# A token-mixing and expert layer pair in fp32: no receptance for the context, two-bank evictions and a 64x64 transposition in the recurrence

## What is computed

```
pc = modulate(rmsnorm(ctx, norm1_g[l]), csh1, csc1) @ w_in[l]
px = modulate(rmsnorm(x, norm1_g[l]), sh1, sc1) @ w_in[l]
cr, ck, cv, cw, ca, cgl = split_rwkv(pc_rw, shift_mu[l], seq_shift(pc_rw))
xr, xk, xv, xw, xa, xgl = split_rwkv(px_rw, shift_mu[l], grid_shift(px_rw, rows))
yc, sf, sb, rc, kc, vc = rwkv_bidir(cr, ck, cv, cw, ca, ..., s_zero, s_zero)
yx, _, _, rx, kx, vx = rwkv_bidir(xr, xk, xv, xw, xa, ..., sf, sb)
def step(s, inp):                     # 8 heads of 64, forwards and backwards
    r_t, w_t, k_t, v_t, a_t, b_t = inp
    sa = einsum('bhvk,bhk->bhv', s, a_t)
    s = s * w_t[:, :, None, :] + sa[..., :, None] * b_t[:, :, None, :] + v_t[..., :, None] * k_t[:, :, None, :]
    return s, einsum('bhvk,bhk->bhv', s, r_t)
```

## Time and profile before

| | us |
|---|---|
| median of the 3 runs shown | 2326.87 |
| lowest, highest | 2322.07, 2332.89 |
| span of the profiled execution | 2324.3 |
| PE busy in it | 2102.2 (90%) |
| VectorE busy | 1575.8 (68%) |
| ScalarE busy | 1245.2 (54%) |
| projection's products, first to last | 60 to 406 |
| recurrence, first logits to last output | 410 to 853 |

### The profile page before, as it was taken

One profiled execution on the slowest core, in us unless ns is written; L12 is line 12 of the kernel. 1 busy time (PEld: TensorE's weight loads), 2 busy tenths in 40 slices (PEclk: granted clock), 3 DMA queues, 4 the chain that ended last, 5 costly groups with the idle time before them and its releaser, 6 DMA issues. The chain is left out here.

```text
span 2324.3 us, 51473 instructions
## 1 busy us (share of the span) xinstructions
PE 2102.2 (90%) x21654; PEld 1675.4 (72%) x21654; DVE 1575.8 (68%) x2324; ACT 1245.2 (54%) x2324; POOL 659.5 (28%) x465
## 2 busy tenths in 40 slices
PE   5999999599999988891799999999958999999989
PEld 3788888477888853681688888888747778866667
DVE  3666654788889746427599999999766846556531
ACT  4422221476677654433688888888645434357530
POOL 0000020566666610114013323323034455400011
PEclk8999999799999999996899999999979999999999
DMA  8222252333222239426599999999845364230032
GB/s 287 59 68 61 71 130 47 74 72 72 64 64 65 58 110 354 146 100 235 208 354 384 389 397 388 387 395 392 280 132 179 105 221 115 88 131 2 2 110 81
DMA packets 164658, 399.63 MB, mean 172 GB/s; under 512 B 13630, under 2 KB 58060, under 8 KB 164428
## 3 DMA queue, kind: packets, MB, share of 16 engines
q1 hardware_dynamic: 149804, 347.56, 43.0%
q0 software_dynamic: 12224, 44.57, 7.0%
q10 hardware_dynamic: 2400, 4.21, 0.5%
HBM read 348.06 MB, written 46.66 MB: 170 GB/s over the span
## 5 line engine op out<-in xcount | busy, mean ns | idle before, releaser
L1940 DVE TENSOR_TENSOR exp_w_lo<-mixT,exp_w_hi 128x2048 fp32r<-128x2048 f32 x124 | 278.7, 2283 | 23.4 <-ACT exp_w_hi L1897 23.4
L1897 ACT ACTIVATE exp_w_hi<-mixT 128x1024 fp32r<-128x1024 f32 x256 | 255.0, 1053 | 55.8 <-PE banks L1859 38.6
L2153 POOL TENSOR_TENSOR w_lo<-mixT,w_hi 128x512 fp32r<-128x512 f32 (+1 forms) x108 | 145.7, 1370 | 166.6 <-ACT w_hi L2229 163.9
L1859 PE MATMUL banks<-exp_w_hi,xsT_lo 128*128 128x512 f32 x512 | 161.0, 396 | 6.3 <-DVE xsT_lo L1944 6.3
L1859 PE MATMUL banks<-exp_w_lo,xsT_hi 128*128 128x512 f32 x512 | 159.4, 393 | 0.0
L1859 PE MATMUL banks<-exp_w_hi,xsT_hi 128*128 128x512 f32 x512 | 159.3, 393 | 0.0
L1827 POOL DMA_INDIRECT moe_rows<-exp_out,idxT x16 | 25.2, 1573 | 435.7 <-DVE exp_out L1999 435.7
L2211 PE MATMUL banks<-w_hi,h_lo 128*128 128x512 f32 (+1 forms) x320 | 123.5, 386 | 7.8 <-POOL w_lo L2153 5.3
L2211 PE MATMUL banks<-w_lo,h_hi 128*128 128x512 f32 (+1 forms) x320 | 120.3, 376 | 0.0
L2211 PE MATMUL banks<-w_hi,h_hi 128*128 128x512 f32 (+1 forms) x320 | 120.2, 376 | 0.0
L1812 POOL DMA_INDIRECT xs<-xn_rows,idxT x16 | 116.0, 7248 | 14.2 <-DVE idxT L1971 5.6
(11 more groups left out here) (395 smaller groups left out, 5857.7 us busy)
## 6 DMA issues: line engine op xcount, KB each, us to landing
mixT<-in_exp_w_up_dram SPq DMA_DIRECT2D x62, 1024.0 KB, 10.2
mixT<-in_exp_w_gate_dram SPq DMA_DIRECT2D x34, 1024.0 KB, 9.3
mixT<-in_exp_w_down_dram SPq DMA_DIRECT2D x32, 1024.0 KB, 9.2
mixT<-in_w_in_dram SPq DMA_DIRECT2D x96, 256.0 KB, 2.9
ada_w_second<-in_ada_w_dram SPq DMA_DIRECT2D x16, 1024.0 KB, 9.6
kaT<-in_exp_w_down_dram SPq DMA_DIRECT2D x16, 1024.0 KB, 7.1
exp_w<-in_exp_w_down_dram SPq DMA_DIRECT2D x16, 1024.0 KB, 7.4
chunk<-rkv_scratch SPq DMA_DIRECT2D x80, 192.0 KB, 4.0
```

The costliest lines, as they stand in the source:

```text
L1859: mm = pe.matmul(g.ps[bank + q][:, :], lhs[:, kk, :], wide[:, k, q * 512:(q + 1) * 512], start=(kk == 0 and p == 0), stop=(kk == KT - 1 an ...
L1897: last = act.activation(wh[:, n % RH, k, :], w[n % RING][:, k, :], ACT.Copy)
L1940: dve.tensor_tensor(wl[:, n % RH, :, :], w[n % RING], wh[:, n % RH, :, :], ALU.subtract).then_inc(lo_ok, 1)
L2153: pool.tensor_tensor(wl[:, q % SR, 0:width(q)], w[:, q % WR, 0:width(q)], wh[:, q % SR, 0:width(q)], ALU.subtract).then_inc(w_lo, 1)
```

## The change

Five edits, of which the first has two halves:

- r (tiles 0 to 3) and the gate's tile 13 are projected, mixed and stored for the image alone; in the recurrence, chunks of the context load, multiply and mask no r.
- `turned` on PE is 16 products of `y` by a 64x64 identity, into both banks of `Q`, 256 columns each, in place of 4 transpositions of 128x128.
- VectorE's `level` and `gram` and ScalarE's `inverse` and `end_columns` take two PSUM banks with one instruction; `turned` on ScalarE reads both banks too.
- `chunk_end` moves from VectorE to ScalarE, between `turned(h, 3)` and `inverse(h, 3)`.
- the state after the last chunk is not made (`fade`, `carry`, `new_state`), and loads of r-less chunks wait for another semaphore.

```diff
+    def rows_of_ctx(kind, j):
+        return kind == "rw" and 4 <= j < 13
...
-                        if kind == "rw":
+                        if rows_of_ctx(kind, j):
                             pe.matmul(g.ps[a][:, 0:TC], lhsT, rhs[:, k, 0:TC], **at)
...
             def chunk(s):
+                kinds = slice(0, 3, 1 if s >= NCC else 2)
...
             for h in TURNS:
-                if inside(h - 1):
+                if inside(h - 1) and inside(h):
                     fade(h - 1)
...
-                act.activation(v.t[:, :, :, :].rearrange("p j d t -> p (j d t)"), v.Q[0][:, :], ACT.Copy).then_inc(act_done[s % 2], 1)
+                act.activation(v.t[:, :, :, :].rearrange("p j d t -> p d j t"), v.bothQ[:, :, 0:W].rearrange("p d (j t) -> p d j t", t=C),
+                               ACT.Copy).then_inc(act_done[s % 2], 1)
...
-                for i in range(2):
-                    ins = act.activation(v.y[:, i::2, :], heads(v.Q[i][:, 0:W]), ACT.Copy)
-                ins.then_inc(act_done[s % 2], 1)
+                act.activation(v.y[:, :, :].rearrange("p (j i) t -> p i j t", i=2), v.bothQ[:, :, 0:W].rearrange("p i (j t) -> p i j t", t=C),
+                               ACT.Copy).then_inc(act_done[s % 2], 1)
...
+            def chunk_end(s):
+                v = group[s % 2]
+                act.wait_ge(exp_done[s % 2], th(s))
+                for d in range(2):
+                    ins = act.activation(v.end[s // 2 % 2][HALVES[d], :], v.gx[HALVES[d], :, 0 if d else C - 1], ACT.Copy)
+                ins.then_inc(ends_ok[s % 2], 1)
...
                 if inside(h):
                     turned(h, 3)
+                if inside(h + 2):
+                    chunk_end(h + 2)
+                if inside(h):
                     inverse(h, 3)
...
-                for i in range(2):
-                    ins = dve.tensor_tensor(v.w[:, i], heads(v.P[i][:, 0:W]), lev, ALU.mult)
-                ins.then_inc(dve_done[s % 2], 1)
+                dve.tensor_tensor(v.w[:, :], v.bothP[:, :, 0:W].rearrange("p d (h t) -> p d h t", t=C), lev, ALU.mult).then_inc(dve_done[s % 2], 1)
...
                 if p == 0:
                     pe.wait_ge(pool_done[s % 2], at("pool", s, "b"))
-                    pe.wait_ge(r_ok[s % 2], th(s))
+                    if s >= NCC:
+                        pe.wait_ge(r_ok[s % 2], ny(s))
...
+                kinds = slice(0, 3, 1 if s >= NCC else 2)
...
+                        mm = pe.matmul(banks[d][:, 3 * j * C:3 * (j + 1) * C].rearrange("p (a t) -> p a t", a=3)[:, kinds],
+                                       v.bk[HALVES[d], n, d:d + 2].rearrange("p a t -> p (a t)"),
+                                       v.are[s // 2 % 2][HALVES[d], n, kinds], start=True, stop=True)
...
                 for j in range(HP):
-                    mm = pe.transpose(v.Q[0][:, j * P:(j + 1) * P], v.y[:, 2 * j:2 * j + 2].rearrange("p j t -> p (j t)"), g.c("ident"))
+                    for par in range(2):
+                        for d in range(2):
+                            mm = pe.matmul(v.Q[d][HALVES[par], j * C:(j + 1) * C], v.y[HALVES[d], 2 * j + par], g.c("eye")[HALVES[d]],
+                                           start=True, stop=True)
                 mm.then_inc(pe_done[s % 2], 1)
...
-                if inside(h - 1):
+                if inside(h - 1) and inside(h):
                     carry(h - 1)
```

More of the change, by code:

```diff
@@ L295, in _ @@
                 pool.wait_ge(mixed, n + 1)
-                pool.dma_start(scr[j // 4 + 1, j % 4], mix[:, q % MR, :].rearrange("p (c t) -> p c t", t=C)).then_inc(stored[q % MR], 16)
+                first = 0 if rows_of_ctx("rw", j) else NCC
+                pool.dma_start(scr[j // 4 + 1, j % 4][:, first:NCH, :],
+                               mix[:, q % MR, first * C:TA].rearrange("p (c t) -> p c t", t=C)).then_inc(stored[q % MR], 16)
                 if 4 <= j < 8:
@@ L464, in shift @@
                 src = raw[:, n % RR, :]
-                step(dve.tensor_scalar(dst, src, g.omu[:, j:j + 1], None, ALU.mult))
+                with_ctx = rows_of_ctx("rw", j)
+                used = slice(0 if with_ctx else TC, TA)
+                step(dve.tensor_scalar(dst[:, used], src[:, used], g.omu[:, j:j + 1], None, ALU.mult))
                 s = src[:, TC:TA].rearrange("p (r c) -> p r c", c=GRID)
@@ L680, in phase_wkv @@
             v.bk = sb(nc, ctx, f"bkb{q}", [P, NH, 3, C])
-            v.gram = [sb(nc, ctx, f"gram{q}{d}", [P, NH, 3, C]) for d in range(2)]
+            v.both_gram = sb(nc, ctx, f"gram{q}", [P, 2, NH, 3, C])
+            v.gram = [v.both_gram[:, d] for d in range(2)]
             v.uv = [sb(nc, ctx, f"uv{q}{d}", [P, NH, C]) for d in range(2)]
@@ L730, in _ @@
                 if inside(s + 2):
-                    sp.wait_ge(r_ok[s % 2], th(s))
+                    if s >= NCC:
+                        sp.wait_ge(r_ok[s % 2], ny(s))
+                    else:
+                        sp.wait_ge(ab_ok[s % 2], th(s))
                     chunk(s + 2)
@@ L830, in end_columns @@
                 act.wait_ge(dve_done[s % 2], at("dve", s, f"g{p}"))
[L831 to L835, removed]
+                banks = v.bothP if p % 2 else v.bothQ
+                act.activation(v.both_gram[:, :, 2 * p:2 * p + 2, 2],
+                               banks[:, :, 0:6 * C].rearrange("p d (h a t) -> p d h a t", h=2, a=3)[:, :, :, 2], ACT.Copy).then_inc(act_done[s % 2], 1)
             def take_r0(s):
@@ L939, in gram @@
                 dve.wait_ge(pe_done[s % 2], at("pe", s, f"g{p}"))
[L940 to L945, removed]
+                banks = v.bothP if p % 2 else v.bothQ
+                kinds = 2 if s >= NCC else 1
+                dve.tensor_tensor(v.both_gram[:, :, 2 * p:2 * p + 2, 0:kinds].rearrange("p d h a t -> p d h (a t)"),
+                                  banks[:, :, 0:6 * C].rearrange("p d (h n) -> p d h n", h=2)[:, :, :, 0:kinds * C],
+                                  masks[:, :, 0:kinds * C].unsqueeze(2).to_broadcast([P, 2, 2, kinds * C]), ALU.mult).then_inc(dve_done[s % 2], 1)
             def a_by_b(s):
@@ L987, in sums, with feature_a @@
                 dve.tensor_tensor(v.gx, v.x, v.sw, ALU.add).then_inc(sums_ok[s % 2], 1)
-            def chunk_end(s):
+            def feature_a(s):
                 v = group[s % 2]
                 dve.wait_ge(exp_done[s % 2], th(s))
[L992 to L997, removed]
                 dve.wait_ge(chunk_in[s % 2], 64 * th(s))
```

22 lines of the change are left out of this document (12 added, 10 removed).

## The result

| us | before | after |
|---|---|---|
| median of 4 runs | 2328.11 | 2368.14 |
| lowest, highest | 2322.07, 2332.89 | 2366.46, 2370.27 |
| span of the profiled execution | 2324.3 | 2364.7 |
| projection's products, first start to last start | 345.6 | 334.4 |
| recurrence, first logits to last output | 442.1 | 497.0 |

What follows compares the result with a forecast made beforehand. PE's instruction supply was to bind the recurrence: projection -11.5, prologue -1.0, end -1.1 and recurrence turns +32.0 sum to +18.4 us, time 2345. Range 2304 to 2372; 2335 to 2372 for the forecast alone.

Steps and rivals of the forecast that it cites:

- A packet of 256 instructions can then not be worked off faster than one in 3.6 to 4.0 us: PE in the recurrence: instructions arrive in 16 KB packets, and PE stops at their borders; lower end taken as 3.45.
- The cycle that I read from two packets: PE's fetch: next packet asked for on entering the last fetched, starts 1.2 us later, takes 1.0 to 1.4, usable 1.45 after.
- Rival A: Recurrence: instruction supply stays hidden, turns 1 to 18 gain 0.4 us each; time 2305; chance 0.22.
- B: Recurrence: supply binds at its lower end, 3.45 us a packet; no change, time 2316 to 2335; chance 0.15.
- D: Two-bank reads run slower than two instructions, y takes 0.75 us; +9 on the hidden-supply case, time 2314; chance 0.04.
- C: Recurrence: packets queue behind chunk loads, 4.0 us a packet plus 0.5 a turn; +54, time 2381; chance 0.12.
- I take 3.75 us for a packet: Turns 5 to 16: 6.05 packets at 3.75 make 22.7 us against 20.39, +27.8; price chosen between 3.45 and 4.0.
- turns 1 to 4: Recurrence turns without outputs: 5.55 packets, 20.8 us a turn against 19.88, +3.7 in all.
- the prologue: Start of the recurrence: shorter by 1 us, between 0 and 2, from the first gram's wait, smaller loads and masks.
- Turns 0 and 19, "ring-bound", -0.4 each: First and last turns: the level's chain sets the time, 192 records in 3.44 us being 4.6 a packet; -0.4 us each.
- the ring: Recurrence: one level's chain from z through transposition, ScalarE's copy, join and copies into y to next z, 3.44 us.
- "0.4 a turn" without the limit: Recurrence levels where instruction supply doesn't bind: 0.05 to 0.1 us saved each, 0.4 a turn.

Runs made afterwards that it cites:

- old_turn: The changed kernel with the 4 transpositions of before put back and ScalarE's copy reading one bank again: 2317.4 us, ratio to before 0.9956.
- receptance_only: The kernel before with only the r-less context and without the last carry; old transposition, evictions and chunk_end kept: 2316.91 us, ratio to before 0.9962.
- twice: The changed kernel with each of the 16 products of turned issued twice into the same place: 2473.27 us in one run.
- eight_transposes: The changed kernel with turned as 8 single-pass transpositions of 64x128 into both banks in place of the 16 products: 2324.55 us, ratio to before 0.9996.
- eight_products: The changed kernel with the 16 products of turned made 8 with 128 weight columns: 2361.99 us, ratio to before 1.0142.

## Why the prediction was right in its cause and short in its size

*Cause.* "A packet of 256 instructions can then not be worked off faster than one in 3.6 to 4.0 us" stands as a mean over a stretch: 3.89 and 3.93 in two kernels, 40.8 us of "issue", a loss that comes and goes with the 280 instructions. The cycle that I read from two packets (1.2, then 1.0 to 1.4, then 1.45) is the one that 54 stops show. Rival A (supply hidden, 2305), B and D are out by the time. C is out by its time too (2381, where the highest run took 2370.27), but not wholly by its mechanism: the chunk loads do hold packets up, by 1.0 us a turn where C had 0.5, and its 4.0 for a packet without them was too much. The Trainium skill (Runtime: NRT & Kernel Launch, Instruction fetch mechanics) has the block of 256 right, and this kernel's traces don't agree with "mostly hidden": the fetch is hidden for the most part before, where a block has 4.15 us (4.7 us of "issue" in 244.65), and not after (40.8 in 283.79).

*The step that failed: "I take 3.75 us for a packet".* It is the term "6.05 x 3.75 = 22.7 against 20.39, **+27.8**". Measured: 6.08 packets of 3.89, 23.65 a turn, +39.1. I put the loads' share at 0.025 over the middle of my bounds (3.725); with a quarter of the loads a packet takes 3.73, so the middle was right, and the loads' share is 0.16. That the middle was right is partly luck, since each bound was read from one or two packets. This term is 11.3 of the 22 us that the forecast lacked; turns 1 to 4 are 6.7, turn 19 2.9, and turns 17 and 18, the prologue and turn 0 between 1.2 and 1.5 each. The earlier start of the projection and the rest of the kernel took 3.3 off again.

*Turns 1 to 4: +10.4 where +3.7 was forecast.* At 3.89 their 5.55 packets are 21.6, +6.9. Most of the rest is turn 2, 24.56 us where turns 1, 3 and 4 took 20.98, 21.57 and 22.75. Its stop and the windows around it (the third number from the end is the granted clock):

```profile
479.33 0.57 PE L1186 MATMUL banks<-const,y 64*64 64x64 f32 x23 [2.07 <-issue]
```

```profile
478.00:481.00 3.00, 1.67 (x55) 1.61 (x55) 0.46 (x1) 1.04 (x2) 2.31 (x2) 0.93 0.03 5
481.00:484.00 3.00, 2.22 (x72) 1.92 (x74) 1.38 (x2) 1.62 (x3) 2.31 (x2) 0.50 0.32 90
484.00:487.00 3.00, 3.00 (x80) 2.66 (x72) 1.12 (x2) 0.91 (x3) 0.83 (x1) 0.50 0.30 90
487.00:490.00 3.00, 2.93 (x100) 2.39 (x96) 1.69 (x4) 1.68 (x4) 1.54 (x3) 0.93 0.03 5
```

PE stood for 2.07 us, and soon after had 1.2 GHz until about 487. I had no term for it. That the stop brought the clock down is the order of events and no more.

*Turns 17 and 18: +2.8* where +1.3 was forecast, the packet's price again (5.55 x 3.89 = 21.6; measured 21.53).

*Turns 0 and 19, "ring-bound", -0.4 each: +0.8 and +2.5.* The step was wrong in kind. I divided the ring's level by its own records (192 in 3.44). But in turn 19's first levels r0, solve, carry and outputs stand between, and there PE stopped:

```profile
868.81 1.03 PE L1086 MATMUL banks<-sv,gram 128*64 128x64 f32 x27 [0.69 <-issue]
873.06 0.68 PE L1186 MATMUL banks<-const,y 64*64 64x64 f32 x28 [0.81 <-issue]
877.09 1.09 PE L1114 MATMUL banks<-gram,uv 128*64 128x64 f32 x27 [0.80 <-issue]
```

2.3 us, all but the whole 2.5. In turn 0 PE stopped twice for 0.7 us each, and not at all before. That covers the +0.8; the granted clock doesn't, for it was 0.84 over this turn in both kernels.

*"0.4 a turn" without the limit.* The ring did get shorter, by 0.15 and not 0.06 to 0.08: y's single copy gives 0.06 (old_turn's ring is 3.38, 829.28 to 832.66), turned the other 0.09, where I had given it 0 to 0.02. But the turns before are 97% PE's own work (236.45 of 244.65), and what the evictions save lies beside that. So nothing is left: old_turn and receptance_only differ by 0.5 us.

*Right.* The projection: -11.2 for -11.5, L620 x72. The end: from the last r0 to the last output 5.9 for 7.0, -1.1. chunk_end at 0: 207 ns a copy, inside ScalarE's idle time. VectorE is 71% busy (201.07 of 283.79). The prologue, -1, came to +0.4, just outside its bounds of 0 and -2. The first gram group does start sooner, 4.9 us behind the products for 5.5. But the products start 17.0 behind the logits for 16.5, behind VectorE's bkb, and z 10.9 behind gram for 10.4, behind GpSimd's first inverse. What made those two later is open.

*The sum again, in spans:* projection -11.2, prologue +0.4, turns 0.8 + 10.4 + 39.1 + 2.8 + 2.5 = +55.6, end -1.1, the rest of the kernel -0.6; that is 43.1. The projection also started 2.7 earlier, at 57.5 for 60.2, but kernels with this change start it anywhere from 57.1 to 60.9, so it is no part of it. 40.4, against 2364.7 - 2324.3 = 40.4.

## What to carry to other kernels

Count an engine's instructions as well as its busy time: fp32 products of 64x64 are so short (32 records in 0.65 us) that 256 instructions of them are worked off faster than the next 256 arrive, and from then on every instruction added costs about its share of a packet (here 3.9 us / 256 = 15 ns; 12 from before to after, 18 from after to twice), however little array time it takes. The sign to look for is idle time laid to "issue" in the middle of a group, at distances of 256 instructions. Array time saved in such a stretch can come back as waiting, as in eight_transposes. Fewer instructions help, as long as they don't give it back in array time: eight_products saved 37 us of waits in turns 5 to 16 and paid 23 of them in busy time.

## What was not expected of the hardware

- Two-bank reads by ScalarE and VectorE carry no price of their own: 512 columns from two banks took 598 ns as y, against 595 from one bank, and 256 columns 378 in place of two of 128 at 283. VectorE's mask of 512 columns from two banks took 689, where two of 256 took 415 each.
- A 64x8 copy took 207 ns on ScalarE and 424 on VectorE.
- Data transfers beside it made a packet of instructions dearer by 0.16 us, though its own transfer stayed at 1.1 (one run).
- One stop of 2.07 us for a packet was followed by about 7 us at half the clock, in a stage that before ran at 1.00 throughout (turns 1 to 4).
